# Down projection of a hybrid encoder block: seven block products instead of eight, in four passes of eleven steps

## The chip, the core and the metric

The kernel runs on one NeuronCore of a Trainium2 chip. The metric is the device time of one execution in microseconds (us), and the median of several executions counts.

## What is computed

One layer of a hybrid encoder: norm, input projection, sliding window attention beside a diagonal state space branch, a gated merge, then a gated feed-forward network with a short causal convolution, and a last norm. Everything is float32, 2048 tokens, width 1024, inner width 2816. The change is in the last line of the feed-forward network:

```python
def conv_ffn(h, w_up, conv_w, conv_b, w_down):
    z = causal_dwconv(h @ w_up, conv_w, conv_b)
    val, gate = jnp.split(z, 2, axis=-1)
    return (jax.nn.gelu(gate) * val) @ w_down      # (2048 x 2816) @ (2816 x 1024)
...
x = x + conv_ffn(rms_norm(x, norm_ffn[l]), w_up[l], conv_w[l], conv_b[l], w_down[l])
return rms_norm(x, norm_final)
```

## The kernel before

All tokens are done in two blocks of 1024 (`blk` 0 and 1), one after the other. There is no scheduler: each engine (PE, DVE, ACT, POOL and the SP queue) has its own program, written out by hand in order, and the engines wait for one another through counting semaphores.

**Three products for one.** Each float32 operand is split into a high part (a cast to fp32r) and a low part (the rest), and every product is three matmuls, high times high, high times low and low times high (`three`, lines 418 to 420), each 128x128 by 128x512.

**Up phase.** The product with `w_up` already runs with seven block products for eight. Its 22 periods (one per 128 columns of the value and of the gate) hold 84 matmuls each. POOL casts the high parts (`half`, line 685), DVE makes the weight sums (lines 1530 to 1541), the low parts (`slot_low`, line 1550), the sums that leave PSUM (`c11`, `c22`, `c12`, lines 1596 to 1608), the two side taps of the convolution (`near` and `far`, lines 1617 and 1622) and the gated product (`ff_mul`, line 1627). The result of each period, 128x1024, is stored to `ff` in DRAM. In the order of DVE, `c22` must be out before PE may start its last product of the period, `p4`.

**Down phase.** It computes `ff` times `w_down` with all eight products, in two passes (512 tokens each) of 22 items. An item is one 128-row of `w_down` (`w_raw`, 512 KB, loaded in line 523) and one 128x512 piece of `ff` (256 KB, line 530). POOL casts and subtracts the weights (`split`, lines 642 and 644), ACT casts the values (`down_hi`, line 738), DVE subtracts (`down_low`, line 1631), and PE adds 24 matmuls into the eight PSUM banks. Four items may be ready ahead (`wd`, `ff_hi`, `ff_lo` have four buffers each). The last three items of a pass (`CHUNK`) are done bank by bank, so that DVE can add finished banks to the residual (`down_add`, line 1640, 128x1024 each) while PE goes on.

**Beside the down phase.** After its load for item 7 the SP queue issues the residual (4 MB, from `x2`) and, in block 0, the 4 MB of x for block 1. ACT sums the squares of the new x (line 800) and DVE scales it (`norm_x`, lines 1228 to 1236 and 1263) in two halves, behind items 16 and 18. The last norm (`out_root`, `out_scaled`, line 1252) is done for tiles 0 to 3 in pass 1, and for tiles 4 to 7 of block 1 behind the last matmul.

Of the kernel before, what the change touches and what calls it, by code (L numbers as in the profile page):

```python
# [55 lines left out]
PASSES = 2  # L56
ITEMS = PASSES * FT
UNITS = U_FFN + ITEMS
CHUNK = 3
# [28 lines left out]
def build(nc, A):  # L88

    with ExitStack() as ctx:  # L90
# [67 lines left out]
        wd = [(at(f"wd_hi{i}", a, [D], F32R), at(f"wd_lo{i}", a + 4, [D], F32R)) for i, a in enumerate((96, 104, 128, 136))]  # L158
        ff_raw = [act_hi[:, i, 0:HALF].bitcast(F32) for i in range(4)]
        ff_hi = [act_hi[:, HK + i, 0:HALF] for i in range(4)]  # L160
        ff_lo = [act_lo[:, HK + i, 0:HALF] for i in range(4)]
# [136 lines left out]
        ffr_in = [sem(f"ff_loaded{i}") for i in range(4)]  # L298
        ffhi_done = sem("ff_hi_ready")
        ff_ready = sem("ff_ready")  # L300
        x2_in = [sem(f"ffn_residual_loaded{i}") for i in range(4)]
        d_used = sem("down_item_used")
        dn_done = sem("down_tile_done")
# [47 lines left out]
        def banks(n):  # L351

            return 3 * (n % 2), 3 * (n % 2) + 1, 3 * (n % 2) + 2

# [127 lines left out]
        def _(sp):  # L482
# [36 lines left out]
            def load_down(blk, i, c, k0):  # L519

                sp.wait_ge(raw_free[c % 2], i * 2 + (blk * (UNITS // 2) + U_FFN // 2 + c // 2))
                src = A["wu"][bass.ds(i * 4 + (U_DN + c - k0), 1)].rearrange("u p n -> (u p) n")
                sp.dma_start(w_raw[c % 2][:, :], src).then_inc(raw_in[c % 2], 16)

            def load_ff(blk, i, c, p):

                if not isinstance(i, int) or c >= 4:
                    sp.wait_ge(ff_ready, i * 4 + (blk * ITEMS + c - 3))
                src = A["ff"][bass.ds(i * 4 + (c - p * FT), 1)].rearrange("u p t -> (u p) t")[:, p * HALF:(p + 1) * HALF]
                sp.dma_start(ff_raw[c % 4], src).then_inc(ffr_in[c % 4], 16)  # L530

            def ffn_traffic(blk):
# [12 lines left out]
                def period(i, c):  # L545
                    sp.wait_ge(*item(slot_ready, W22, blk, i, c))
                    load_pair(i, c + 2)
                    if not isinstance(i, int) or c:
                        store_ff(blk, i, c - 1)
                period(0, 0)  # L550
# [5 lines left out]
                load_down(blk, 0, 0, 0)  # L556
                load_down(blk, 0, 1, 0)
                store_ff(blk, 0, FT - 3)
                sp.wait_ge(*item(prod_done, W11, blk, 0, FT - 1))
                for k in range(4):  # L560
                    sp.wait_ge(ff_st[k % 2], 16 * (blk * (FT // 2) + k // 2 + 1))
                    load_ff(blk, 0, k, 0)
# [1716 lines left out]
```

## Time and profile before

| | |
|---|---|
| median of 3 runs | 2584.61 us (2581.55 to 2585.11) |
| the profiled execution | 2581.78 us, span of its instructions 2580.0 us |
| PE busy | 2507.2 us, 97% of the span, 11906 matmuls |
| DVE, ACT, POOL busy | 1527.3, 727.8 and 959.6 us |
| DMA | 298.53 MB, mean 116 GB/s |
| down phase, block 0 and 1 | from 1059 to 1312 us and from 2329 to 2570 us |

The span runs from the first to the last instruction. Matmuls overlap in the pipeline: a row shows some 390 ns for one of 128x512, while one starts every 0.227 us. What the kernel gains or loses is therefore read from the gaps of PE and from the number of its matmuls.

### The profile page before, as it was taken

Reading aid. Unit: us, or ns where it says so; the run is one execution under the profiler, and the core shown is the slowest. Engines: PE = TensorE matmul, PEld = TensorE weight load, DVE = VectorE, ACT = ScalarE, POOL = GpSimd, SP = SyncE. Lnnn points to the kernel's source line nnn. Section 1 sums busy time; section 2 is a strip of 40 time slices with the busy share of each in tenths; the row PEclk is TensorE's granted clock in tenths of the full one; section 3 lists DMA queues with packets and bytes.
Section 4 is the critical chain, followed back from the end, with each engine's and each line's share of the span. In section 5 each row is a group of like instructions: output and inputs, shape, how many; then the busy total and the mean of one; then the engine's idle time right before and its main releaser. Section 6 shows DMA issues by size and latency. Waiting matters only on the chain.

```text
span 2580.0 us, 34191 instructions
## 1 busy us (share of the span) xinstructions
PE 2507.2 (97%) x11906; PEld 2058.2 (80%) x11906; DVE 1527.3 (59%) x2209; ACT 727.8 (28%) x1413; POOL 959.6 (37%) x667
## 2 busy tenths in 40 slices
PE   6999999999999999989999999999999999999998
PEld 5777788888888888868878878888878888888886
DVE  6945455546888888537230235556378888884253
ACT  4035213312333323221121351142133333331111
POOL 2322222350333333567722222225313333336684
PEclk9999999999999999999999999999999999999999
DMA  6242342442121222564412123324312212225452
GB/s 197 88 107 86 131 152 78 147 183 78 66 82 73 89 81 85 183 223 170 147 40 94 54 98 135 127 106 147 155 58 90 81 73 89 81 90 216 147 192 106
DMA packets 117356, 298.53 MB, mean 116 GB/s; under 512 B 18136, under 2 KB 35320, under 8 KB 117256
## 3 DMA queue, kind: packets, MB, share of 16 engines
q1 hardware_dynamic: 79408, 217.37, 23.8%
q10 hardware_dynamic: 37848, 79.80, 8.9%
q8 instruction: 66, 1.08, 0.2%
q14 instruction: 34, 0.28, 0.0%
HBM read 228.45 MB, written 68.68 MB: 115 GB/s over the span
## 4 chain that ended last, share of the span: by engine, by line
PE 87%; DVE 7%; DMA 2%; ACT 2%; POOL 1%; issue 1%; SPq 1%; ACTq 0%; POOLq 0%; DVEq 0%
PE ps L418 27%; PE ps L420 27%; PE ps L419 26%; DMA act_hi<-ff 1%; POOL wd_lo L644 1%; PE ps L1991 1%; PE ps L1977 1%; DVE act_lo L1243 1%; PE ps L1926 1%; PE ps L1915 1%; PE ps L1994 1%; PE ps L1992 1%; PE ps L1837 0%; DVE glu_y L1485 0%; DVE set_t_b L1305 0%
## 5 line engine op out<-in xcount | busy, mean ns | idle before, releaser
L642 POOL CAST w_hi<-w_raw 128x1024 fp32r<-128x1024 f32 x72 | 78.2, 1086 | 744.2 <-PE ps L420 729.2
L685 POOL CAST slot_hi<-pair_raw 128x512 fp32r<-128x512 f32 x220 | 175.9, 804 | 476.0 <-PE ps L420 430.9
L418 PE MATMUL ps<-act_hi,w_hi 128*128 128x512 f32 x832 | 334.3, 402 | 14.4 <-DVE act_lo L1243 7.5
L420 PE MATMUL ps<-act_hi,w_lo 128*128 128x512 f32 x832 | 327.1, 393 | 0.0
L419 PE MATMUL ps<-act_lo,w_hi 128*128 128x512 f32 x832 | 326.2, 392 | 0.0
L418 PE MATMUL ps<-wd_hi,act_hi 128*128 128x512 f32 x704 | 274.7, 390 | 12.1 <-DVE act_lo L1631 12.1
L418 PE MATMUL ps<-act_hi,slot_hi 128*128 128x512 f32 x704 | 274.2, 390 | 0.3 <-DVE slot_lo L1550 0.3
L420 PE MATMUL ps<-wd_hi,act_lo 128*128 128x512 f32 x704 | 274.3, 390 | 0.0
L419 PE MATMUL ps<-wd_lo,act_hi 128*128 128x512 f32 x704 | 274.3, 390 | 0.0
L420 PE MATMUL ps<-act_hi,slot_lo 128*128 128x512 f32 x704 | 273.9, 389 | 0.0
L419 PE MATMUL ps<-act_lo,slot_hi 128*128 128x512 f32 x704 | 273.9, 389 | 0.0
L1631 DVE TENSOR_TENSOR act_lo<-act_hi 128x512 fp32r<-128x512 f32 x88 | 114.4, 1310 | 249.2 <-ACT act_hi L738 249.1
L644 POOL TENSOR_TENSOR wd_lo<-w_raw,wd_hi 128x1024 fp32r<-128x1024 f32 x88 | 236.4, 2687 | 7.0
L418 PE MATMUL ps<-tw_hi,slot_hi 128*128 128x512 f32 x528 | 206.3, 391 | 1.6 <-ACT part L738 1.4
L420 PE MATMUL ps<-tw_hi,slot_lo 128*128 128x512 f32 x528 | 205.5, 389 | 0.0
L419 PE MATMUL ps<-tw_lo,slot_hi 128*128 128x512 f32 x528 | 205.4, 389 | 0.0
L418 PEld LDWEIGHTS ps<-act_hi,w_hi 128*128 128x128 f32 x832 | 157.8, 190 | 51.4 <-DVE act_lo L1243 8.6
L685 POOL CAST slot_hi<-sums 128x512 fp32r<-128x512 f32 x84 | 119.0, 1416 | 206.2 <-DVE sums L1530 108.6
L420 PEld LDWEIGHTS ps<-act_hi,w_lo 128*128 128x128 f32 x832 | 157.7, 190 | 34.4
L644 POOL TENSOR_TENSOR w_lo<-w_raw,w_hi 128x1024 fp32r<-128x1024 f32 x72 | 182.2, 2531 | 5.8
L419 PEld LDWEIGHTS ps<-act_lo,w_hi 128*128 128x128 f32 x832 | 158.0, 190 | 31.2
L418 PEld LDWEIGHTS ps<-wd_hi,act_hi 128*128 128x128 f32 x704 | 132.5, 188 | 40.4 <-DVE act_lo L1631 12.9
(326 smaller groups left out, 4872.4 us busy)
## 6 DMA issues: line engine op xcount, KB each, us to landing
w_raw<-in_wu SPq DMA_DIRECT2D x176, 512.0 KB, 3.5
pair_raw<-in_wu SPq DMA_DIRECT2D x88, 512.0 KB, 3.9
ff<-z SPq DMA_DIRECT2D x44, 512.0 KB, 2.6
act_hi<-ff SPq DMA_DIRECT2D x88, 256.0 KB, 3.7
gates<-junk ACTq DMA_DIRECT2D x64, 256.0 KB, 2.0
sig<-gates ACTq DMA_DIRECT2D x32, 512.0 KB, 4.9
tbl_o<-tables ACTq DMA_DIRECT2D x32, 384.0 KB, 3.4
tbl_r<-tables ACTq DMA_DIRECT2D x32, 256.0 KB, 2.7
```

What stands on the lines that cost most here:

```text
L418: nc.tensor.matmul(out, lh, rh, start=first, stop=False, skip_group_check=onto)
L419: nc.tensor.matmul(out, lh, rl, start=False, stop=False, skip_group_check=onto)
L420: return nc.tensor.matmul(out, ll, rh, start=False, stop=last, skip_group_check=onto)
L642: nc.gpsimd.tensor_copy(hi, w_raw[b][:, :]).then_inc(hi_made, 1)
L644: nc.gpsimd.tensor_tensor(lo, w_raw[b][:, :], f(hi), ALU.subtract).then_inc(w_ready, 1)
L685: nc.gpsimd.tensor_copy(slot_hi[j][:, :, :], src).then_inc(slot_half[KIND[j]], 1)
L1243: stt(act_lo[:, k, cols], ps[:, 4 + n % 4, :], gain[:, k:k + 1], f(act_hi[:, k, cols]), ALU.mult, ALU.subtract).then_inc(act_ready, 1)
L1631: tt(ff_lo[c % 4], ff_raw[c % 4], f(ff_hi[c % 4]), ALU.subtract).then_inc(ff_ready, 1)
L1915: ins = nc.tensor.transpose(ps[:, 6 + j // 4, (j % 4) * P:(j % 4 + 1) * P], logit[i % 2][:, j, :], ident[:, :])
L1926: ins = mm(ps[CH * g:CH * g + CH, 2 + i % 2, par * 256:(par + 1) * 256], vv, rhs, start=True, stop=True)
L1977: ins = mm(ps[SS * g:SS * g + SS, s_bank[m % 2], ri * P:(ri + 1) * P], tbl_r[m % NR][:, TB_W + ri * P + SS * g:TB_W + ri * P + SS * g + SS ...
L1991: mm(o, s_h[b][:, 0, 0:NCH], tab[:, out_v:out_v + 256], start=True, stop=False)
```

## The change

The eight block products of the down phase become seven. The 1024 tokens of a block are split into early and late (512 each), the 22 rows of `w_down` into 11 pairs of an even and an odd row, and its columns into left and right. A **step** is one pair in one pass. With A11, A12 the early values of the even and odd row, A21, A22 the late ones, and B11 to B22 the weights alike:

| pass | steps | products | value sums by DVE | loads of a step |
|---|---|---|---|---|
| 0 | 0 to 10 | A11 B11 and A12 B21 | none | 4 pieces, 1 MB |
| 1 | 11 to 21 | S2 T2 and S1 T1 | S1 = A21 + A22, S2 = S1 - A11 | 5 pieces, 1.25 MB |
| 2 | 22 to 32 | S3 T3 and S4 B22 | S3 = A11 - A21, S4 = A12 - S2, from three operations | 6 pieces, 1.5 MB |
| 3 | 33 to 43 | A22 T4 | none | 2 pieces, 0.5 MB |

A piece is 128x512 (256 KB). The weight sums T1 = B12 - B11, T2 = B22 - T1, T3 = B22 - B12 and T4 = B21 - T2 are the same for both blocks: DVE makes them in the up phase of block 0, two operations behind each period's `slot_low` of the last slot, from rows that SP loads for it, and SP stores them to `tw` in DRAM. The raw buffers of a step are three deep, the operands four deep, and they now lie over all of `act_hi` and `act_lo`. POOL only casts, and DVE makes the low parts of the weights too. Products accumulate in banks 0 to 3 and 4 to 7 through the passes; DVE adds them to the residual in 28 half tiles of 128x512. `CHUNK` is 2, and its unit is now a bank.

```diff
+            def load_step(blk, t):
+                n, j = t // PAIRS_K, t % PAIRS_K
+                b = t % 3
+                if t >= 3:
+                    sp.wait_ge(step_ready, operands_by(blk, t - 3))
...
+                for dst, src in pairs:
+                    sp.dma_start(dst, src).then_inc(step_in[b], 16)
...
+                def down_t(i, c):                       (SP, up phase of block 0)
...
+                    if c:
+                        sp.wait_ge(t_done, i * 4 + 2)
+                        store_t(i, 1)
+                        store_t(i, 2)
+                    elif not isinstance(i, int) or i:
+                        sp.wait_ge(t_done, i * 4)
+                        store_t(i - 1, 0)
+                        store_t(i - 1, 3)
+                        sp.wait_ge(t_st, i * 64)
...
+                        load_t(i, c)
...
+                sp.wait_ge(*item(prod_done, S1, blk, 0, FT - 1))
+                load_step(blk, 0)
+                sp.wait_ge(*item(prod_done, S3, blk, 0, FT - 1))
+                load_step(blk, 1)
+                load_step(blk, 2)
...
+                    load_step(blk, t)
+                    if blk + 1 < BLOCKS and 5 <= t < 9:
+                        load_x(sp, blk + 1, t - 5, t - 4)
+                    if 9 <= t < 13:
+                        j = t - 9
+                        sp.dma_start(xres[:, 2 * j:2 * j + 2, :], x2[:, 2 * j:2 * j + 2, :]).then_inc(x2_in[j], 16)
...
+                for t in range(STEPS):                  (POOL)
+                    if t == 0:
+                        pool.wait_ge(*item(prod_done, W12, blk, 0, FT - 1))
+                    elif t == 2:
+                        pool.wait_ge(*item(prod_done, W22, blk, 0, FT - 1))
+                    elif t >= 4:
+                        pool.wait_ge(d_used, blk * STEPS + t - 3)
+                    pool.wait_ge(step_in[t % 3], loads_by(blk, t))
+                    for n in range(products(t)):
+                        nc.gpsimd.tensor_copy(d_hi[t % 4][n], raw_w[t % 3][:, n, :]).then_inc(d_half, 1)
...
+                def step_lows(t):                       (DVE)
+                    value_sums(t + 1)
+                    for n in range(products(t)):
+                        dve.wait_ge(d_half, halves_by(blk, t) - products(t) + n + 1)
+                        tt(d_lo[t % 4][n], raw_w[t % 3][:, n, :], f(d_hi[t % 4][n]), ALU.subtract).then_inc(step_ready, 1)
...
+                        tt(f_lo[t % 4][n], value_of(t, n), f(f_hi[t % 4][n]), ALU.subtract).then_inc(step_ready, 1)
...
+                for t in range(3, STEPS):
+                    step_lows(t)
+                    if blk + 1 < BLOCKS and t in (7, 9):
+                        norm_x(blk + 1, (t - 7) // 2)
+                    if t in (12, 23, 34):
+                        for n in range(8 * (t // PAIRS_K) - 8, 8 * (t // PAIRS_K)):
+                            bank_add(n)
+                    if t == 36:
+                        out_root(blk, 0, 4, out_parts(blk))
+                    if 36 <= t < 40:
+                        out_scaled(t - 36)
```

**DVE, behind the last slot of an up period.** Before (`slot_lo_148` is the low part of the fourth sum, the two z rows are `near` and `far`):

```order
L1608 TENSOR_TENSOR pre_157<-part_155,ps 128x512
L1550 TENSOR_TENSOR slot_lo_148<-pair_raw_152,slot_hi_141 128x512
L1617 SCALAR_TENSOR_TENSOR z_159<-pre_157,conv_v_185,z_159 128x1024
L1622 SCALAR_TENSOR_TENSOR z_159<-pre_157,conv_v_185,z_159 128x1024
```

and with the change, in block 0 (`down_t_row` and `down_t_164` hold the rows of `w_down`):

```order
L1680 TENSOR_TENSOR pre_157<-part_155,ps 128x512
L1622 TENSOR_TENSOR slot_lo_148<-pair_raw_152,slot_hi_141 128x512
L1708 TENSOR_TENSOR down_t_row<-down_t_row 128x512
L1709 TENSOR_TENSOR down_t_row<-down_t_164,down_t_row 128x512
L1689 SCALAR_TENSOR_TENSOR z_159<-pre_157,conv_v_186,z_159 128x1024
L1694 SCALAR_TENSOR_TENSOR z_159<-pre_157,conv_v_186,z_159 128x1024
```

Two operations of 128x512 have come in between `slot_low` and `near`.

**DVE, one and a half steps of pass 2, with the change** (`step_f` and `step_w` are the raw values and weights of a step, a number of the buffer behind them; before, an item had one row here, `act_lo<-act_hi`):

```order
L1728 TENSOR_TENSOR step_f_168<-step_f_168 128x512
L1729 TENSOR_TENSOR step_f_168<-step_f_168 128x512
L1731 TENSOR_TENSOR step_f_168<-step_f_168 128x512
L1737 TENSOR_TENSOR act_lo<-step_w_170,act_hi 128x512 x2
L1740 TENSOR_TENSOR act_lo<-step_f_167,act_hi 128x512 x2
L1728 TENSOR_TENSOR step_f_166<-step_f_166 128x512
```

The three sums of the next step (buffer 168) stand ahead of the four low parts of this one (buffers 170 and 167).

## Rows read from the trace of the kernel before

**Rows 1.** Page, costliest groups: busy us, mean ns, idle before and its releaser

```profile
L418 PE MATMUL ps<-wd_hi,act_hi 128*128 128x512 f32 x704 | 274.7, 390 | 12.1 <-DVE act_lo L1631 12.1
L1631 DVE TENSOR_TENSOR act_lo<-act_hi 128x512 fp32r<-128x512 f32 x88 | 114.4, 1310 | 249.2 <-ACT act_hi L738 249.1
```

**Rows 2.** Timeline of ACT, two items: start, length, idle before

```profile
1164.82 0.63 ACT L738 ACTIVATE act_hi<-act_hi 128x512 fp32r<-128x512 f32 x1 [3.37 <-PE ps L420]
1170.26 0.63 ACT L738 ACTIVATE act_hi<-act_hi 128x512 fp32r<-128x512 f32 x1 [4.81 <-PE ps L420]
```

**Rows 3.** Stretches of 4 us, block 0: PE, PEld, DVE, ACT, POOL, PEclk, DMA, GB/s

```profile
1100.00:1104.00 4.00, 2.92 (x13) 2.07 (x12) 0.00 (x0) 0.00 (x0) 0.00 (x0) 1.00 1.03 410
1104.00:1108.00 4.00, 0.00 (x0) 0.00 (x0) 0.00 (x0) 0.00 (x0) 0.00 (x0) 0.85 1.02 408
...
1112.00:1116.00 4.00, 1.88 (x5) 1.49 (x6) 3.51 (x2) 0.63 (x1) 3.56 (x3) 0.50 0.32 99
```

**Rows 4.** Chain of waits, block 0: start, length, what

```profile
1095.75 14.82 DMA act_hi<-ff
...
1115.34 0.43 PE ps L420
```

**Rows 5.** Stretches of 4 us, block 1, same columns

```profile
2373.00:2377.00 4.00, 3.14 (x15) 2.39 (x14) 2.50 (x2) 0.13 (x1) 3.57 (x3) 1.00 0.52 189
```

**Rows 6.** Operations by line: ns min, median, max; first and last start

```profile
L1550 DVE TENSOR_TENSOR slot_lo<-pair_raw,slot_hi x220: 671/681/1104, 563.3 to 2317.6; 128x512 fp32r<-128x512 f32 x110
L685 POOL CAST slot_hi<-sums x84: 617/1478/1485, 648.1 to 2303.1; 128x512 fp32r<-128x512 f32 x84
```

**Rows 7.** DMA issues by line: KB each, median us to landing

```profile
w_raw<-in_wu SPq DMA_DIRECT2D x176, 512.0 KB, 3.5
pair_raw<-in_wu SPq DMA_DIRECT2D x88, 512.0 KB, 3.9
ff<-z SPq DMA_DIRECT2D x44, 512.0 KB, 2.6
```

**Rows 8.** Timelines of DVE and ACT around the norm of the new x

```profile
1147.11 1.04 ACT L800 ACTIVATE junk<-xnext 128x1024 bf16<-128x1024 f32 x1
1148.26 1.28 ACT L738 ACT_TABLE_LOAD   x1
1148.27 0.17 DVE L1228 TENSOR_SCALAR var_x<-ssq_x 128x4 f32<-128x4 f32 x1 [2.60 <-ACT junk L800]
1152.77 5.74 DVE L1263 TENSOR_SCALAR xnext<-xnext,rstd_x 128x1024 f32<-128x1024 f32 x4
```

**Rows 9.** Operations by line: the scaling of x, ns min, median, max

```profile
L1263 DVE TENSOR_SCALAR xin<-xin,rstd_x x12: 745/749/2879, 14.5 to 1166.5; 128x1024 f32<-128x1024 f32 x12
```

**Rows 10.** Timelines of the up phase: DVE and SP in one period

```profile
808.16 0.36 SPq L517 DMA_DIRECT2D ff<-z  x1
811.00 0.69 DVE L1603 TENSOR_TENSOR pre<-part,ps 128x512 f32<-128x512 f32 x1 [0.78 <-issue]
814.43 0.69 DVE L1550 TENSOR_TENSOR slot_lo<-pair_raw,slot_hi 128x512 fp32r<-128x512 f32 x1
816.07 1.28 DVE L1617 SCALAR_TENSOR_TENSOR z<-pre,conv_v,z 128x1024 f32<-128x1024 f32 x1 [0.94 <-ACT z L1083]
```

**Rows 11.** A stretch of 50 us of the up phase, columns as in rows 3

```profile
800.00:850.00 50.00, 50.00 (x223) 41.39 (x222) 42.72 (x54) 15.23 (x26) 18.22 (x19) 1.00 0.25 94
```

**Rows 12.** Timeline of PE: its last matmul of the down phase

```profile
2569.86 0.39 PE L420 MATMUL ps<-wd_hi,act_lo 128*128 128x512 f32 x1
```

**Rows 13.** Timeline of DVE behind it: last add, its norm, last scaling

```profile
2570.36 1.22 DVE L1640 TENSOR_TENSOR xres<-xres,ps 128x1024 f32<-128x1024 f32 x1 [0.21 <-PE ps L420]
2571.50 0.15 DVE L1228 TENSOR_SCALAR var_out<-ssq_out 128x1 f32<-128x1 f32 x1
2574.14 0.15 DVE L1228 TENSOR_SCALAR var_out<-ssq_out 128x1 f32<-128x1 f32 x1
2575.58 1.28 DVE L1252 SCALAR_TENSOR_TENSOR xres<-xres,rstd_out,gfin 128x1024 f32<-128x1024 f32 x1
```

More of the change, by code:

```diff
@@ L55 @@
 U_DN = U_UP + 2 * FT
[L56 to L59, printed above, removed]
+UNITS = U_FFN
+PAIRS_K = FT // 2
+PASSES = 4
+STEPS = PASSES * PAIRS_K
+CHUNK = 2
 W11, W12, S1, S2, S3, S4, W22 = range(7)
@@ L1148, in period @@
                     else:
-                        for k in range(4):
-                            down_hi(0, k)
+                        value_hi(0)
                     value_out_pair(i, c)
@@ new lines, in value_sums @@
+                def value_sums(t):
+                    if t >= STEPS or not sums_of(t):
+                        return
+                    made = sums_by(blk, t)
+                    a, b, c, d = (raw_f[t % 3][:, n, :] for n in range(4))
+                    dve.wait_ge(step_in[t % 3], loads_by(blk, t))
+                    if sums_of(t) == 2:
+                        tt(a, a, b, ALU.add).then_inc(step_sum, 1)
+                        dve.wait_ge(step_sum, made + 1)
+                        tt(c, a, c, ALU.subtract).then_inc(step_sum, 1)
+                    else:
+                        tt(a, a, c, ALU.subtract).then_inc(step_sum, 1)
+                        tt(b, b, d, ALU.subtract).then_inc(step_sum, 1)
+                        dve.wait_ge(step_sum, made + 2)
+                        tt(b, b, a, ALU.add).then_inc(step_sum, 1)
@@ L1858, in proj @@
                         pe.wait_ge(proj_evac, blk * 2 * N_IN + (3 if n == 3 else n - 1))
+                    if blk and n < 3:
+                        pe.wait_ge(dn_evac, blk * ADDS)
                     if n in (12, 13):
@@ L2195, in _, with down_bank @@
-                for c in range(FT + 1, 24):
-                    down_item(0, c)
-                with pe.Fori(6, 10) as i:
-                    for c in range(4):
-                        down_item(i, c)
-                for c in range(40, ITEMS - CHUNK):
-                    down_item(0, c)
-                down_last(1)
+                def down_bank(t, n, q, first, last):
+                    tok = slice(q * P, (q + 1) * P)
+                    b = t % 4
+                    return three(ps[:, 4 * n + q, :], f_hi[b][n][:, tok], f_lo[b][n][:, tok], d_hi[b][n], d_lo[b][n],
+                                 first, last, onto=t // PAIRS_K not in ((0,), (0, 1))[n])
```

356 lines of the change are left out of this document (176 added, 180 removed).

## The prediction

> **What bounds the kernel now.** I read the page first: PE is busy for 97% of the span, so time can only come from fewer matmuls or from PE's gaps. Then the groups: all waits of PE ahead of the down phase's matmuls come to 12.1 us, and DVE's 88 low parts stand idle for 249 us waiting for casts [rows 1]. So in the down phase everything but PE waits, and PE sets the pace. That pace is read off ACT, whose cast waits until PE has freed a buffer: one item every 1170.26 - 1164.82 = 5.44 us [rows 2]. An item has 24 matmuls, so one matmul starts every 0.2267 us.
>
> The gaps come next. In block 0 DMA runs at 408 to 410 GB/s while PE stops at 1102.9 us [rows 3]. The chain names a single transfer of values, 14.8 us long: it is queued behind the 8 MB of residual and new x [rows 4]. Of the 12.1 us, 0.9 belong to block 1 [rows 5], so 11.2 to this gap. Behind it the granted clock reads 0.50, that is 1.2 GHz [rows 3], and matmuls take 0.43 us each [rows 4], which costs about 2 us more.
>
> **What goes.** Before, 2 x 1056 matmuls; now 33 steps of 24 and 11 of 12, 924 a block. So 264 fewer: 264 x 0.2267 = **59.8 us**. The gap of 11.2 us, its 2 us of slow clock and the 0.9 us of block 1 go too (**14.1 us**), since x and residual are now loaded 1 MB at a time between step loads. From step 5 to 12 a step asks for 2.1 to 2.4 MB, 5.1 to 5.8 us at 410 GB/s against 5.44; the steps by then ready cover that.
>
> **What comes: the work of DVE.** A subtraction of 128x512 takes 0.68 us, pipelined 0.61, and up to 1.10 us when it meets a cast of POOL; the cast takes 0.62 us at least and 1.48 us when it meets DVE [rows 6]. So the two take turns: I count them as one resource. The Trainium skill (SBUF — State Buffer, section on the shared port pair) says so too: a DVE operation with two SBUF inputs and a GpSimd operation exclude each other for a whole instruction. By the rows alone they could still miss one another in part, and that is the lower bound below.
>
> A step of pass 1 is 6 DVE operations and 2 casts: 6 x 0.61 + 2 x 0.6 = 4.9 us, with two dependent waits 5.2. Pass 2 has 7 operations: 5.8 at worst, 5.2 if some casts fall into gaps. There is a second tie. `value_sums(t + 1)` stands ahead of the low parts of step t, and the load of step t + 1 starts only when step t - 2 is ready. So two steps cost one landing plus one step of DVE. A 512 KB load lands in 3.5 us [rows 7], of which 1.3 are transfer at 410 GB/s, so 2.2 are fixed; 1.31 MB land in 5.4 us, 1.57 MB in 6.0. The period is (5.4 + 5.4)/2 = 5.4 us in pass 1 and (6.0 + 5.5)/2 = 5.7 in pass 2, where PE wants 5.44. And at the end of each pass DVE also adds eight half tiles (8 x 0.65, 5 us) while its next step waits. For eleven steps DVE needs 11 x 5.4 + 5 = 64.4 us in pass 1 and, with some of the adds under landings, about 65 in pass 2; PE needs 59.8. The last two steps of a pass must both be ready, so lead is eaten there. That is 4.6 and 5 us a block, **19 us** in all, waited mostly ahead of steps 20 and 31. Nearest bound below: casts in the gaps, 0. Bound above: 0.75 us for each operation and a step on every landing, 15 us a block. I take the middle, as every piece of it has a row.
>
> **The head.** Before, four items could be ready. Now steps 2 and 3 lie over operands that PE reads until its last up product, and step 1 loads only when the S3 product is done, 5.6 us ahead of step 0 (two products of 12 matmuls). It lands at -1 us, but DVE still has `ff_mul`, `c12`, `near` and `far` of the last period between the low parts of steps 0 and 1: about 5.5 us, then four low parts. Stepping the order forward gives step 1 ready at 8.8 us in block 0 (with its two T sums) and 7.6 in block 1, where PE asks at 5.4: **5.6 us** together. At best 1, at worst 8.
>
> **The norm of the new x, block 0.** One half is four squares of ACT (1.04 us each, with their reads 1.13), a table load of 1.28 us the first time, six small DVE operations, and four scalings that took 5.74 us beside POOL's subtractions [rows 8] but take 0.75 us each alone [rows 9]. So a half holds DVE for 4.3 us, and the first for 8 with the wait for ACT. Before, DVE idled 2.8 us an item on average (249.2/88, [rows 1]). Now both halves stand inside steps 7 to 10, after the loads of x have used up the lead (step 7 is ready only some 2 us early). From step 7 to 10 DVE needs 8 + 4.3 + 3 x 2.8 + 1.4 us of sums = 22 us; PE, wanting 9 and 10 together, gives it 2 + 2 x 5.44 = 13. **10 us** of waiting, ahead of steps 8 and 9; bounds 5 and 15.
>
> **Clock.** A gap of 7 us is likely to bring the slow clock again: it cost 2 us behind the gap of 11 [rows 3, 4]. I put 3 us for all gaps; bounds 0 and 8.
>
> **The tail.** Before, PE's last matmul ends at 2570.1 [rows 12] and the span 9.9 us later: one add of 1.22 us, two norms of 2.64 us, a store [rows 13]. Finished tiles came 4.08 us apart (18 matmuls). Now they come 1.36 us apart (6 matmuls), and a norm still takes 2.64. With E the end of PE: adds at E - 4.0 and E - 2.6, norm until E + 0.7, add, norm until E + 4.0, add, norms until E + 7.3 and E + 9.9, store 3.1. The tail is 13.0: **+3.1 us**.
>
> **The up phase of block 0.** Two operations of DVE come into each of 22 periods of 84 x 0.2267 = 19.0 us. They stand ahead of `near`, which waits 0.94 us there anyway [rows 10]. In even periods they wait for rows that SP loads only after its stores of sums have landed: SP is free at 808.5, two stores more land by 812.2 (512 KB land in 2.6 us [rows 7]), the rows 4.2 us later at 816.4, where DVE would ask at 815.1 [rows 10]. So `near` moves by 1.7 us. Behind it DVE waits 0.78 us ahead of `c22` [rows 10], and PE wants `c22` only after one more product, 2.7 us, of which `c22` takes 0.69. Slack 2.8, need 1.7: hidden; **2 us** for jitter and the first period, bounds 0 and 8. The additional traffic, 2 MB in two periods, 55 GB/s, runs beside 94 GB/s [rows 11] and costs nothing.
>
> **Sum.** Profiled execution 2581.8 us: - 59.8 - 14.1 + 19 + 5.6 + 10 + 3 + 3.1 + 2 = - 31.2, so 2550.6. That execution lies 2.8 us below the median of the runs, so I say **2551 us**. A measurement of this kernel tells 0.2% (5 us) from no change.
>
> A page speaks against the change. Rows show reads at 408 to 410 GB/s [rows 3]. The Trainium skill (DMA: Bandwidth & Descriptors, "Where 436 GB/s comes from") says that between HBM and SBUF some 360 GB/s bind. By its figure the 1.57 MB alone would take 4.4 us, an estimate, and the sum would come out near rival 2.
>
> **Rivals.**
> 1. *All cover holds* (0.14). Casts fall between DVE's operations, so only the norm (9 us) and 2 us of the head are left: 2581.8 - 73.9 + 11 + 1 + 3 + 1 = 2524. For it: DVE has a median of 0.68, not 0.9, in the up phase beside POOL [rows 6].
> 2. *The loads are the bound* (0.18). Values and weights come in rows of 2 KB instead of 4, three to four transfers a step. If a landing takes 0.6 to 0.8 us longer, both passes' periods grow by 0.35 us: 22 steps in each of two blocks, 15 us, and 2 more at the norm: 2568. For it: steps 5 to 12 already need 94% and more of the time at 410 GB/s. Against: nothing else is in the queue in pass 2.
> 3. *Slower, through the up phase* (0.07). If the rows land 2 us later than I said, DVE's wait for them delays `c22` past its 2.8 us of slack, and PE stands in `p4`. It decides from a delay of `near` of 3 us on, and to end above 2590 it has to cost 1.8 us in each of 22 periods. DVE is then busy or blocked for over 19.0 us a period; it was busy 42.72 of 50, so 16.2 [rows 11], and the two operations add 1.3.
> 4. *Slower, through DVE in passes 1 and 2* (0.04). It decides from 0.8 us an operation on (every third meets a cast and waits it out): a step takes 6.0 us in pass 1 and 6.8 in pass 2, with the adds 11 and 20 us a block over PE, less 4 of lead, so 54 in place of 19: 2586.
>
> That the change does not do what it says is not open: the matmuls are counted in the program.
>
> **Numbers.** The forecast has 0.57, with a range of its own from 2538 to 2562. Range for 8 in 10: 2528 to 2574, from half of rival 1 to beyond rival 2. Faster 0.88, within 0.2% 0.04, slower 0.08.
>
> **What would show it.** PE: 11642 matmuls, the last one some 13 us ahead of the end. Waits of PE for DVE `act_lo` of 2 to 4 us ahead of step 1, 2 to 10 ahead of steps 8 and 9 of block 0, about 3 ahead of steps 20 and 31 in both blocks. DVE idle in pass 2 until `step_f` lands; `step_f` landing in 5.5 to 6 us. The up phase of block 0 as long as that of block 1 to 2 us. It is wrong if PE waits in the up phase, if DVE's operations in the down phase average over 0.8 us, or if passes 1 and 2 run without a gap.

## The result, and the profile after

The changed kernel takes 2570.44 us (median of 6 runs, 2566.25 to 2574.32), the kernel before in the same job 2584.86 us (6 runs, 2581.55 to 2587.49). The ratio is 0.994, with a 95% interval from 0.9927 to 0.9953. So it is faster by 14.4 us, where 33.6 had been forecast; the time lies inside the range of 2528 to 2574, near its upper end. The profiled execution took 2574.16 us, its span 2572.0. In the job of the last four kernels below one execution of the kernel before took 5130.5 us; it is left out of their ratios.

The first two parts of the page:

```profile
span 2572.0 us, 33476 instructions
PE 2470.1 (96%) x11642; PEld 2020.2 (79%) x11642; DVE 1714.0 (67%) x2623; ACT 760.8 (30%) x1479; POOL 771.6 (30%) x645
```

PE has the 11642 matmuls of the forecast. The waits of PE in the down phase of block 0 (1071.9 to 1312.5 us) and then of block 1 (2330.2 to 2558.9), by the view of waits (who waited, for what: us in total, times, longest):

```profile
PE ps L466 <- DVE act_lo L1740: 20.1, 5, 7.3
...
PE ps L466 <- DVE act_lo L1740: 11.7, 4, 6.2
PE ps L466 <- DVE xres L1756: 1.8, 1, 1.8
```

Before, all such waits came to 12.1 us [rows 1]; now they are 33.6. Of these 31.8 are for the last low part of a step, and 1.8, ahead of step 11 of block 1, for DVE's add (`xres`) that empties the bank which step 11 writes. I placed each by the starts of PE's matmuls (a step is 24 of them, 12 in pass 3). A stop is a stretch between two starts that is over 0.3 us longer than 0.2267, and it counts with what it is longer:

| | block 0 | block 1 |
|---|---|---|
| down phase before | 252.2 | 240.5 |
| after | 240.5 | 228.7 |
| of it matmuls at 0.2267 us | 209.5 | 209.5 |
| stops in all | 22.3 | 14.7 |
| ahead of step 1 | 3.6 | 1.7 |
| ahead of steps 8 to 11 | 7.8 | 2.9 |
| ahead of step 20 | 6.7 | 6.7 |
| ahead of steps 30 and 31 | 4.2 | 3.4 |
| starts at double distance | 7.7 | 3.4 |

The last row is what starts some 0.43 us apart cost over 0.2267; smaller delays make up the missing 1.0 and 1.1 us. The starts at double distance come behind the stops, as here behind the one ahead of step 20 (stretches of 4 us: busy us and count of PE, PEld, DVE, ACT, POOL, then PEclk, DMA share, GB/s):

```profile
1192.00:1196.00 4.00, 4.00 (x20) 3.30 (x19) 2.34 (x4) 0.76 (x2) 0.00 (x0) 1.00 0.93 336
1196.00:1200.00 4.00, 0.54 (x3) 0.11 (x1) 2.50 (x3) 0.00 (x0) 2.08 (x2) 0.94 0.95 325
1200.00:1204.00 4.00, 1.26 (x3) 1.10 (x4) 4.00 (x7) 1.15 (x2) 1.63 (x2) 0.50 0.23 72
1204.00:1208.00 4.00, 4.00 (x14) 3.12 (x14) 3.72 (x6) 1.15 (x2) 0.08 (x1) 0.71 0.98 334
```

After a stop of 6.4 us the granted clock is 0.50, that is 1.2 GHz, and still 0.71 on average in the next stretch: 14 matmuls in 4 us in place of 18.

Why the low parts are late shows in DVE's timeline, for the step of pass 1 behind a load and for the first sums of pass 2 (start, length, idle before and its releaser):

```profile
1184.93 0.69 DVE L1724 TENSOR_TENSOR step_f<-step_f 128x512 f32<-128x512 f32 x1 [1.72 <-DMA step_w<-tw]
1185.65 0.98 DVE L1726 TENSOR_TENSOR step_f<-step_f 128x512 f32<-128x512 f32 x1
1186.56 1.69 DVE L1737 TENSOR_TENSOR act_lo<-step_w,act_hi 128x512 fp32r<-128x512 f32 x2
1188.18 1.28 DVE L1740 TENSOR_TENSOR act_lo<-step_f,act_hi 128x512 fp32r<-128x512 f32 x2
...
1197.46 0.69 DVE L1728 TENSOR_TENSOR step_f<-step_f 128x512 f32<-128x512 f32 x1 [3.13 <-DMA step_w<-in_wu]
```

and in SP's, which issues a load as soon as a step is ready:

```profile
1178.43 0.88 SPq L587 DMA_DIRECT2D step_f<-ff  x2
1179.35 0.43 SPq L587 DMA_DIRECT2D step_w<-tw  x1
...
1189.48 0.88 SPq L587 DMA_DIRECT2D step_f<-ff  x2
```

The load issued at 1178.43 is waited for until 1184.93, 6.5 us; then come two sums and four low parts, and at 1189.48 the step is ready and SP issues the load of the next step but two. That is the two-step tie of the prediction: 11.05 us for two steps, 6.5 of landing and 4.55 of DVE, 5.5 a step, where PE takes 5.44. In pass 2 the issues lie (1259.98 - 1223.94)/6 = 6.0 us apart. The landing had been put at 5.4 us. Two things in the trace go with the difference, and no run separates them: the third transfer is issued 0.92 us behind the first (1178.43 and 1179.35), and the rate climbs slowly. Stretches of 1 us around the issue at 1156.56, whose data DVE takes up at 1162.96:

```profile
1157.00:1158.00 1.00, 1.00 (x6) 0.84 (x5) 0.97 (x3) 0.05 (x1) 0.00 (x0) 1.00 0.41 49
1158.00:1159.00 1.00, 1.00 (x7) 0.81 (x6) 1.00 (x3) 1.00 (x2) 0.00 (x0) 1.00 0.80 172
1159.00:1160.00 1.00, 1.00 (x6) 0.84 (x5) 1.00 (x3) 0.11 (x1) 0.00 (x0) 1.00 1.00 326
1160.00:1161.00 1.00, 1.00 (x6) 0.82 (x5) 0.27 (x1) 0.00 (x0) 0.00 (x0) 1.00 1.03 379
```

Two more places. In the up phase of block 0 PE now waits for `c22` (L1675), and DVE for the rows of the weight sums; the view of waits from 660 to 1071 us:

```profile
PE ps L466 <- DVE pre L1675: 3.8, 7, 0.7
...
DVE down_t_row L1708 <- DMA down_t<-in_wu: 28.5, 10, 3.3
```

That up phase takes 438.5 us; before it took 432.1, as the one of block 1 does in both kernels. By the starts of the matmuls 6.1 of the 6.4 us are stops of 0.1 to 1.0 us in nine periods, none of them in two periods running. And the tail: the last matmul starts at 2558.67, and DVE's last scaling is here, where [rows 13] had 2575.58:

```profile
2558.67 0.39 PE L468 MATMUL ps<-act_hi,act_lo 128*128 128x512 f32 x1
```
```profile
2567.61 1.28 DVE L1324 SCALAR_TENSOR_TENSOR xres<-xres,rstd_out,gfin 128x1024 f32<-128x1024 f32 x1
```

The parts add up. Down phases: -23.5; up phase of block 0: +6.4; tail 13.1 us in place of 9.9: +3.2; between the phases -0.5. That is -14.4, the difference of the medians. (Ahead of the first up phase the profiled execution is 6.3 us longer than the one before, though the program is the same there; with it the two spans differ by 8.0 us. Over all kernels below that phase starts between 626.8 and 634.2 us, so it is left out of the sum. That the rest meets the difference of the medians so exactly is in part chance.)

### The profile page after: what moved, and what is told of

The parts are those of the page before. It is cut to its first block, busy times and chain, and to the rows that moved or that the text cites. A ratio compares the mean times of both kernels' runs of the same rounds, so it can differ in the third digit from the quotient of the medians.

```text
span 2572.0 us, 33476 instructions
## 1 busy us (share of the span) xinstructions
PE 2470.1 (96%) x11642; PEld 2020.2 (79%) x11642; DVE 1714.0 (67%) x2623; ACT 760.8 (30%) x1479; POOL 771.6 (30%) x645
## 4 chain that ended last, share of the span: by engine, by line
PE 68%; DVE 17%; DMA 7%; issue 3%; ACT 2%; SPq 1%; POOL 1%; DVEq 0%; ACTq 0%; POOLq 0%
PE ps L466 21%; PE ps L468 20%; PE ps L467 20%; DMA step_w<-in_wu 3%; DMA step_w<-tw 2%; DVE act_lo L1737 2%; DVE act_lo L1740 2%; DMA down_t<-in_wu 1%; SPq L587 1%; DVE slot_lo L1622 1%; PE ps L2097 1%; DVE act_lo L1315 1%; PE ps L2083 1%; DVE z L1699 1%; POOL slot_hi L764 1%
## 5 line engine op out<-in xcount | busy, mean ns | idle before, releaser
L764 POOL CAST slot_hi<-pair_raw 128x512 fp32r<-128x512 f32 x220 | 183.8, 842 | 419.5 <-PE ps L468 325.0
L466 PE MATMUL ps<-act_hi 128*128 128x512 f32 x616 | 247.1, 401 | 33.6 <-DVE act_lo L1740 31.8
L467 PE MATMUL ps<-act_lo,act_hi 128*128 128x512 f32 x616 | 244.8, 397 | 0.0
L468 PE MATMUL ps<-act_hi,act_lo 128*128 128x512 f32 x616 | 244.1, 396 | 0.0
L805 POOL CAST act_hi<-step_w 128x512 fp32r<-128x512 f32 x154 | 139.0, 926 | 341.4 <-DMA step_w<-in_wu 155.3
L813 ACT ACTIVATE act_hi<-step_f 128x512 fp32r<-128x512 f32 x154 | 89.4, 624 | 329.0 <-DVE step_f L1731 101.0
L466 PEld LDWEIGHTS ps<-act_hi 128*128 128x128 f32 x616 | 118.6, 193 | 64.9 <-DVE act_lo L1740 38.9
```

The lines of the kernel that those rows point to most:

```text
L466: nc.tensor.matmul(out, lh, rh, start=first, stop=False, skip_group_check=onto)
L467: nc.tensor.matmul(out, lh, rl, start=False, stop=False, skip_group_check=onto)
L468: return nc.tensor.matmul(out, ll, rh, start=False, stop=last, skip_group_check=onto)
L764: nc.gpsimd.tensor_copy(slot_hi[j][:, :, :], src).then_inc(slot_half[KIND[j]], 1)
L805: nc.gpsimd.tensor_copy(d_hi[t % 4][n], raw_w[t % 3][:, n, :]).then_inc(d_half, 1)
L813: ins = nc.scalar.activation(out, in_, kw.pop("func", ACT.Identity), **kw)
```

## The experiments

Three questions: what makes the waits in passes 1 and 2 (the tie, the landings, DVE's work or its meeting with POOL); what makes those ahead of steps 8 and 9; what makes the first up phase longer. Ratios are to the kernel before, run in the same job; the phases are from each run's trace, to be held against 240.5 and 228.7 us for the down phases and 438.5 for the up phase.

**No weight sums.** `down_t` is not called and the step loads take plain rows of `w_down`, so the weight sums are left out of the computation.

```
-                    if blk == 0:
-                        down_t(i, c)
...
-(raw_w[b][:, :, :], tmade[:, 0:2, :])
+(raw_w[b][:, :, :], wide[:, :, HALF:])
```

> Leaves out the weight sums T1 to T4: their loads, their DVE operations and their stores in the up phase of block 0, and every step loads plain rows of w_down of the same size instead (so the down products are of other weights). Theory A (the loads of those rows land after DVE asks for them, so DVE is late for c22 and PE waits 0.5 to 0.9 us in every second period): the up phase of block 0 falls from 438.5 us to the 432.1 us of block 1, its seven gaps of PE inside the loop go, the head of the down phase of block 0 waits 1.5 us less at step 1, and the whole is 6 to 9 us faster than the change. Rival (the two operations themselves fill DVE, or the stores disturb the loads of the next pair): the same sum, but then PE's gaps would not stand in every second period alone. Both phases down are otherwise as they are: PE waits at steps 8, 9, 20 and 31.

Measured: 2554.64 us (4 runs, 2549.78 to 2558.19), ratio 0.9877 (0.9854 to 0.99). The up phase of block 0 is back at 432.2: the sums and what hangs on them cost the whole 6.4 us there. The down phases take 233.6 and 226.9, with 3.3 and 6.0 us ahead of step 20 (6.7 in both blocks with the sums), 3.3 and 2.8 ahead of step 31 and 8.0 ahead of step 9. So the waits of passes 1 and 2 do not hang on the rows in DRAM that hold the sums, though the one ahead of step 20 of block 0 is halved: a load issued at 1158.36 is taken up at 1164.37, 6.0 us later in place of 6.4 to 6.5, and two steps take 10.6 us in place of 11.05.

**Casts on ACT.** The 154 casts of a step's weights are made by ACT in place of POOL.

```
-                        nc.gpsimd.tensor_copy(d_hi[t % 4][n], raw_w[t % 3][:, n, :]).then_inc(d_half, 1)
+                        copy(d_hi[t % 4][n], raw_w[t % 3][:, n, :], d_half, 1)
```

> The casts of the weights in the down phase are done by ACT ahead of those of the values; POOL does nothing there. Theory B (DVE's operations with two inputs in SBUF and POOL's casts take turns, and that makes a step of passes 1 and 2 longer than PE's 5.44 us): DVE's low parts of the weights fall from 0.84 us mean to 0.64, PE's waits ahead of steps 20 (6.4 us in both blocks) and 31 (3.3) go, steps 8 and 9 of block 0 keep 7 to 9 us, the slow clock costs 2 to 4 us in place of 11: 22 to 30 us faster than the change, ratio to before 0.983 to 0.986. Rival C (the landing of the loads sets the period, DVE's length does not matter): waits at 20 and 31 stay within 1 us, under 6 us faster. Rival D (ACT becomes late instead, four casts of 0.63 us and its own waits): PE waits for ACT or for DVE behind ACT, no gain.

Measured: 2548.31 us (4 runs, 2545.45 to 2552.07), ratio 0.9854 (0.9835 to 0.9873); down phases 231.7 and 218.7. Ahead of step 20 stand 1.6 us in both blocks, ahead of step 31 2.6 and 2.5, and 2.1 and 1.9 are new ahead of step 22, where PE waits for the adds that empty its banks. DVE by line, from 1126 to 1260 us in the changed kernel (two rows), and from 1120 to 1260 with the casts on ACT (two rows); busy us and mean ns, then idle before and its releaser:

```profile
L1729 DVE TENSOR_TENSOR step_f<-step_f 128x512 f32<-128x512 f32 x10 | 9.7, 972 | 0.0
L1728 DVE TENSOR_TENSOR step_f<-step_f 128x512 f32<-128x512 f32 x10 | 7.3, 729 | 11.0 <-DMA step_w<-in_wu 11.0
```
```profile
L1721 DVE TENSOR_TENSOR step_f<-step_f 128x512 f32<-128x512 f32 x11 | 7.6, 692 | 0.4
L1718 DVE TENSOR_TENSOR step_f<-step_f 128x512 f32<-128x512 f32 x11 | 7.6, 691 | 15.6 <-DMA step_w<-in_wu 15.6
```

The second sum falls from 0.97 to 0.69 us. The Trainium skill (SBUF — State Buffer, "Who interferes with whom") says that a DVE instruction with two SBUF inputs contends with a GpSimd instruction that reads SBUF. That fits: without POOL's casts every group of DVE's sums and low parts has a mean of 0.68 to 0.69 us here. But DVE does not stop waiting for loads; it idles longer before them (15.6 us in place of 11.0 on that line). A shorter step of DVE shortens the circle of landing and step; that this is the way in which it helps is my reading, and the order of sums moved below bears it out.

**Four deep.** A fourth buffer for a step's raw values and weights; a load waits for the step four back. POOL's weight splits of block 1 wait until the last step of block 0 is ready, since the buffer lies over theirs.

```
-(96, 128, 136))]
+(96, 128, 136, 184))]
...
-                if t >= 3:
-                    sp.wait_ge(step_ready, operands_by(blk, t - 3))
+                if t >= 4:
+                    sp.wait_ge(step_ready, operands_by(blk, t - 4))
```

> A fourth raw buffer for the values and weights of a step (in the place of the weight buffers that the down phase does not use), so that the load of step t waits for step t - 4 and not t - 3. Nothing else. Theory C (value_sums(t + 1) stands ahead of the low parts of step t, so that with three buffers two steps cost one landing and one step of DVE): the waits at steps 20 and 31 of both blocks go, 9 us a block with what the clock adds, about 20 us faster than the change. Theory B alone (DVE and POOL need over 5.44 us a step whatever the loads do): the waits shrink by under a third, under 7 us faster. If both are needed at once, since the period is their sum, this and the run with the casts on ACT each take the waits away.

Measured: 2538.42 us (4 runs, 2537.07 to 2541.68), ratio 0.9818 (0.98 to 0.9836); down phases 226.1 and 212.7. No stop is left ahead of steps 20 and 31 in either block; ahead of steps 8 and 9 of block 0 there are still 2.1 and 6.5 us. So DVE, with all its operations and its meetings with POOL, keeps up with PE in passes 1 and 2 once it need not wait for loads.

**The last four steps bank by bank.** In pass 3 four steps share a bank in place of two, so that tiles finish farther apart.

```
+                    chunk = 4 if p == 3 else CHUNK
-                    if t % PAIRS_K < PAIRS_K - CHUNK:
+                    if t % PAIRS_K < PAIRS_K - chunk:
```

> In pass 3 alone the last four steps are done bank by bank, in place of the last two, so that finished banks come 2.72 us apart and not 1.36. Theory (the tail of 13.1 us is DVE's row of norms, 2.64 us a tile with an add of 0.6, that starts late): DVE has done two norms by the end of PE, the tail falls to about 10.5 us, 2 to 3 us faster than the change. Rival (four steps must be ready at once at step 40, which PE waits for): the gain is eaten by a new wait of 2 to 5 us ahead of step 40 in both blocks, so slower by up to 6 us.

Measured: 2583.08 us (10 runs, 2575.62 to 2588.02), ratio 0.999 (0.9977 to 1.0002). The tail falls from 13.1 to 10.4 us (tiles now 12 matmuls apart), but PE stops 4.7 and 4.9 us ahead of step 40 in block 0 and 1: all four steps must be ready at once. The last of them, step 43, waits for its load and not for a free operand. In block 0 PE has left step 39's operands at 1301.5; the load, issued at 1300.34 when step 40 was ready, releases POOL's cast at 1303.82. The tail's 2.7 us cost 9 and more.

**Weight sums behind near and far.**

```
-                    if blk == 0:
-                        down_t(i, c)
                     near(0, i, c)
                     far(0, i, c)
+                    if blk == 0:
+                        down_t(i, c)
```

> The two DRAM-bound weight sums of a period stand behind near and far on DVE in place of ahead of them; nothing else is changed. My theory: the first up phase is 6.4 us longer than the second because the sums wait ahead of near for their rows, and near pushes c22 past its slack. Then the up phase of block 0 falls from 438.5 to 432 to 433 us, and the time from 2570 to about 2564. Rival: the two more operations or the 2 MB more of traffic in two periods cost the time by themselves, wherever they stand; then the up phase of block 0 stays at 437 to 439 us and the time at 2570.

Measured: 2565.28 us (4 runs, 2560.59 to 2569.16), ratio 0.9912 (0.9889 to 0.9935); up phase of block 0 433.2 us. The same operations and the same traffic cost 1.1 us in place of 6.4. The view of waits from 660 to 1067 us: PE now waits once for `c22`.

```profile
PE ps L466 <- DVE pre L1675: 0.8, 1, 0.8
```

**Sums of values behind the low parts.** One line of DVE's order is moved.

```
                 def step_lows(t):
-                    value_sums(t + 1)
                     for n in range(products(t)):
...
                         tt(f_lo[t % 4][n], value_of(t, n), f(f_hi[t % 4][n]), ...)
+                    value_sums(t + 1)
```

> On DVE the sums of values of step t + 1 stand behind the low parts of step t in place of ahead of them; nothing else is changed. My theory: in passes 1 and 2 the load of step t + 1 starts only when step t - 2 is ready, and step t is ready only when step t + 1 has landed, so that two steps cost a landing of 6.4 us and a step of DVE. With that tie cut the waits of PE ahead of steps 20 and 31 shrink from 6.4 and 3.3 us in each block to under 2 each, and the wait ahead of step 9 of block 0 shrinks too: 2554 to 2560 us. Rival: DVE has too much to do in these passes beside the casts (six or seven operations a step, eight adds at the end of a pass). Then the waits stay within 1 us of what they were and the time at 2567 to 2571.

Measured: **2533.70 us** (4 runs, 2532.42 to 2538.84), ratio 0.9802 (0.9781 to 0.9824), 20 us better than the best that I had expected. The down phases take 223.5 and 212.0 us, stops 10.0 and 1.9 us, starts at double distance 3.3 and 0. Waits of PE in the down phase of block 0, then block 1:

```profile
PE ps L466 <- DVE act_lo L1739: 8.7, 3, 4.7
...
PE ps L466 <- DVE act_lo L1739: 1.5, 1, 1.5
```

DVE's timeline in pass 2, one step:

```profile
1187.02 0.68 DVE L1728 TENSOR_TENSOR step_f<-step_f 128x512 f32<-128x512 f32 x1
1187.62 0.68 DVE L1729 TENSOR_TENSOR step_f<-step_f 128x512 f32<-128x512 f32 x1
1188.33 0.69 DVE L1731 TENSOR_TENSOR step_f<-step_f 128x512 f32<-128x512 f32 x1
1189.53 1.67 DVE L1736 TENSOR_TENSOR act_lo<-step_w,act_hi 128x512 fp32r<-128x512 f32 x2 [0.51 <-POOL act_hi L805]
1191.12 1.28 DVE L1739 TENSOR_TENSOR act_lo<-step_f,act_hi 128x512 fp32r<-128x512 f32 x2
1192.33 0.68 DVE L1728 TENSOR_TENSOR step_f<-step_f 128x512 f32<-128x512 f32 x1
```

A step takes 1192.33 - 1187.02 = 5.3 us, and DVE never waits for a load. From 1124 to 1246 us the first sums of both passes stood idle for

```profile
L1724 DVE TENSOR_TENSOR step_f<-step_f 128x512 f32<-128x512 f32 x11 | 9.2, 833 | 1.9 <-DMA step_w<-tw 1.9
L1728 DVE TENSOR_TENSOR step_f<-step_f 128x512 f32<-128x512 f32 x11 | 9.1, 830 | 0.0
```

1.9 us, where the changed kernel has 21.8 (10.8 on L1724 and 11.0 on L1728, 1126 to 1260 us). The landings are no shorter: by the view of DMAs a 512 KB transfer of `step_f` takes 5.1 us here and 4.7 there. So for the waits ahead of steps 20, 30 and 31 the tie was the cause, and no resource. The down phases hold 33.7 of the some 36 us gained. With the sums ahead, the low parts of step t wait for load t + 1, which is issued when step t - 2 is ready; the three buffers work like two. With the sums behind, they wait for load t, issued when step t - 3 is ready.

**Norm later.** Its halves stand at steps 14 and 18 on ACT and DVE.

```
-                    if blk + 1 < BLOCKS and t in (7, 9):
+                    if blk + 1 < BLOCKS and t in (14, 18):
```

> The two halves of the norm of the new x stand at steps 14 and 18 in place of 7 and 9, for ACT and DVE both; the loads stay where they are. The forecast's theory: the norm holds DVE while PE waits ahead of steps 8 and 9 of block 0. Then the wait of 7.5 us ahead of step 9 falls under 2 us and, with its slow clock, the time by about 9 us to 2561, unless the norm then costs the same ahead of step 20. Rival: the wait comes from the 8 MB of x and residual between the step loads of steps 5 to 12. Then 5 to 7 us stay ahead of steps 8 to 10, the wait ahead of step 20 of block 0 grows by 2 to 4 us, and the time is 2568 to 2575.

Measured: 2575.28 us (7 runs, 2568.22 to 2578.38), ratio 0.9952 (0.9936 to 0.9969), no better than the changed kernel. The wait ahead of step 9 is 9.3 us in place of 7.8, with no norm near it, and 3.2 us come in ahead of steps 19 and 22. The norm was not what stopped PE at step 9; the rival holds.

**Loads spread, norm later.** As before, and the eight loads of 1 MB stand ahead of steps 5, 7, ... 19.

```
-                    if blk + 1 < BLOCKS and 5 <= t < 9:
+                    if blk + 1 < BLOCKS and t in (5, 7, 13, 15):
...
-                    if 9 <= t < 13:
+                    if t in (9, 11, 17, 19):
```

> As the run before, and the eight loads of 1 MB of x and residual stand in front of every second step (5, 7, 9, 11, 13, 15, 17, 19) in place of eight steps in a row. If the burst of loads makes the wait ahead of step 9, it falls under 2 us here and not in the run before, and the down phase of block 0 becomes 8 to 12 us shorter than that of the changed kernel (240.5): 2560 us. If the norm alone made it, this run and the one before are alike. A part may come back ahead of step 20, where loads of pass 1 now share the queue with x.

Measured: 2563.15 us (4 runs, 2562.56 to 2567.65), ratio 0.9916 (0.9895 to 0.9936), down phase of block 0 236.8 us. The wait ahead of step 9 falls from 9.3 to 4.0. That part of it is the burst of loads; what is left had not been expected.

**Both orders.** 

> Both moves of DVE's order together: the sums of values of step t + 1 behind the low parts of step t, and the two DRAM-bound weight sums behind near and far. The two causes lie in different phases, so the gains should add: the down phases as with the first move alone (223.5 and 212.0 us), the up phase of block 0 at 433 us as with the second alone; 2533.7 - 5 = about 2528.5 us. Rival: with the first up phase shorter the stores of sums run into the next loads and a part comes back; over 2532.

Measured: 2537.42 us (4 runs, 2535.02 to 2537.7), ratio 0.9806 (0.9785 to 0.9827). The up phase of block 0 takes 433.2 us, as expected, the down phases 225.2 and 212.2; yet the time is that of the order of sums alone, within the interval. In the two traces the 5.3 us gained in the up phase stand against 6.9 us more ahead of it (the phase starts at 633.7 us here and at 626.8 there), where the programs are the same, and 1.7 us in the down phase of block 0, where the wait ahead of step 1 is 5.2 us in place of 2.8. The 6.9 us lie in the first 200 us, and the granted clock differs there. The same stretch of 4 us with the sums alone moved, then with both:

```profile
134.00:138.00 4.00, 2.88 (x14) 2.21 (x13) 3.97 (x2) 1.36 (x3) 0.00 (x0) 1.00 0.71 231
```
```profile
134.00:138.00 4.00, 4.00 (x21) 4.00 (x20) 3.93 (x3) 2.48 (x5) 1.44 (x1) 0.50 0.38 109
```

One program takes several times there, so a gain of 5 us can hide in the start of an execution; that it varies between executions of one kernel, and not between kernels, is likely but not shown, as each was traced once.

**Loads spread and the head moved, on top.** The two moves just tried, and step 1's casts and low parts (`value_hi(1)`, `step_lows(1)`) ahead of `near` and `far` of the last period.

> As the run before, and three moves more: the loads of x and residual in front of every second step from 5 to 19, the two halves of the norm at steps 14 and 18, and step 1's casts and low parts ahead of near and far of the last period. Left in the down phase of block 0 are the waits ahead of step 1 (2.8 us), of steps 8 and 9 (1.5 and 4.9) and 3.3 us of slow clock. If those at 8 and 9 come from the burst of loads they go, and with them the slow clock: down phase of block 0 at 212 to 214 us, the time at 2517 to 2520. If it is the norm, they move to steps 15 to 19: 2525 to 2529.

Measured: 2536.38 us (4 runs, 2529.61 to 2538.35), ratio 0.9798 (0.9771 to 0.9825): nothing gained. Both waits moved. The one ahead of step 1 (5.2 us in block 0) is now ahead of step 2 (4.9). Step 2's load is not late (issued at 1061.46, step 0 starts at 1065.9) and its casts are done by 1072.1; but in DVE's order its low parts stand behind `near`, `far` and the weight sums, and end at 1081.4. Those ahead of steps 8 and 9 are gone, and 6.6 us stand ahead of steps 19 to 22, where the norm and the late x loads are; 2.8 of them are waits for the adds of pass 1, which DVE reaches late. With three buffers and POOL's casts the new x costs about 6 us in block 0 wherever it is put.

**The last three steps bank by bank, on top.** As the run with four, with 3.

> As the run before, and in pass 3 of a block the last three steps run bank by bank in place of two, so that finished tiles come 9 matmuls apart (2.0 us) in place of 6 (1.4). If the order of DVE's sums was what made the steps of pass 3 late in the run with four such steps, no new wait comes ahead of step 41 and the tail falls from 13.1 to about 11.8 us: 1 to 1.5 us less than the run before. If loads are late by themselves there, a new gap of 2 us or more ahead of step 41 in both blocks makes it 2 to 5 us longer.

Measured: 2538.73 us (4 runs, 2537.16 to 2542.87), ratio 0.9812 (0.9791 to 0.9833). New stops of 2.7 and 2.0 us ahead of step 41 in both blocks, though DVE's order is mended. The load is the limit here too. Step 43's, into one of three raw buffers, is issued at 1279.08; PE has left the operands of step 39 at 1280.06; and POOL's cast for step 43 waits for the load:

```profile
1283.42 0.61 POOL L806 CAST act_hi<-step_w 128x512 fp32r<-128x512 f32 x1 [2.69 <-DMA step_w<-tw]
```

**Four deep and casts on ACT, on top of the spread loads.**

> As the run with spread loads and the moved head, and a fourth buffer for a step's loads and the casts of weights on ACT in place of POOL. If what was wrong with passes 1 and 2 was the tie of two steps alone, nothing is left there for a buffer or for a free port to give: within 0.1% of that run. If a little of the wait ahead of steps 8 and 9 is left there, up to 3 us less.

Measured: **2521.23 us** (4 runs, 2518.97 to 2522.76), ratio 0.9749 (0.9727 to 0.977), the best of all. Down phases 212.9 and 210.1 us of which 209.5 are matmuls. All that is left of PE's waits in them, block 0:

```profile
PE ps L466 <- DVE act_lo L1731: 2.0, 2, 1.3
```

I had expected 0 to 3 us less than with spread loads alone; it is 15, of which 11.7 in block 0 and 3.4 in block 1. Two things were changed at once, but where the time goes shows in DVE's rows. Ahead of step 2 stand 1.5 us in place of 4.9, and step 2's load is issued no earlier than before (4.3 us ahead of step 0 here, 4.4 there). What is shorter is DVE's work: from the start of step 0's low parts to the end of step 2's it takes 15.5 us in place of 18.4, with POOL's casts gone from beside it. Step 2's low parts of the weights, with spread loads alone and here:

```profile
1078.12 2.11 DVE L1737 TENSOR_TENSOR act_lo<-step_w,act_hi 128x512 fp32r<-128x512 f32 x2
```
```profile
1072.91 1.29 DVE L1728 TENSOR_TENSOR act_lo<-step_w,act_hi 128x512 fp32r<-128x512 f32 x2
```

Around the second half of the norm it is the same: from the sums ahead of it to the adds of pass 1 DVE takes 27.7 us in place of 31.2 (1157.30 to 1184.99, 1167.30 to 1198.50), and in neither run does it wait more than 0.4 us for loads there. So once the order is mended and the loads are spread, DVE's time sets the wait in the head and behind the norm, and there its meetings with POOL cost. What the fourth buffer gives beside that, no run shows alone.

## Why the prediction was wrong, and where it was right

By its own steps, in us, measured from the same two traces. The mechanisms were mostly right, and two terms were far too small: the slow clock (+3, measured +11.1) and the up phase of block 0 (+2, measured +6.4).

| step | forecast | measured |
|---|---|---|
| 264 fewer matmuls | -59.8 | -59.8 (239.4 to 209.5 a block) |
| gap of before, its clock, block 1 | -14.1 | -13.7 |
| DVE and loads in passes 1 and 2 | +19 | +21.0 (steps 20, 30, 31) |
| head, step 1 | +5.6 | +5.3 |
| norm of the new x | +10 | +7.8 at steps 8 and 9, +2.9 in block 1 |
| slow clock | +3 | +11.1 |
| tail | +3.1 | +3.2 |
| up phase of block 0 | +2 | +6.4 |
| small ones | 0 | +1.4 |
| sum | -31.2 | -14.4 |

**The clock** is the step that failed most: 8 of the 16.8 us. I priced it as one gap, from the 2 us behind the gap of 11 us [rows 3, 4], and added one for the rest. By the starts at double distance, the stops of the changed kernel brought 2.4 us (behind the stop of 3.2 us at step 1), 1.2 (behind 7.5), 1.6 (behind 6.4) and 2.4 (behind 3.3) in block 0, and 2.0 (behind 6.4) and 1.4 (behind 3.4) in block 1; those of 0.6 to 2 us brought none. A stop of 3 us had the price of one of 7, and the one of 11 before had 1.0, where the prediction had read 2. So the number of longer stops counted, not their sum. The down phases of all 14 traces say so too: none of 51 stops of 0.5 to 1.95 us brought any; of 36 between 1.95 and 3.5 us 13 brought none and the others 0.2 to 2.4; each of 30 longer ones brought 1.0 to 2.4, and those of over 6 us no more than those of 3.5 to 6. With the order of sums mended, 10.0 us of stops bring 3.3 us of it in block 0, and 1.9 us none in block 1. Behind the term stands a second slip: it was made for gaps as a whole, while the waits had been forecast one by one, at seven places.

**The up phase** was mis-sized by 4.4 us. The mechanism stands in rival 3: the rows come late, `near` moves, `c22` misses its slack. The slack was taken as 2.8 us; in the changed kernel DVE's wait for the rows takes 2.9 us on average over ten periods and up to 3.3, where `near` had been forecast to move by 1.7, and PE then stops for `c22` in every second period. The move behind `far` shows that the place was the cause.

**Passes 1 and 2** came out near the sum, by luck of two errors. The landing of pass 1 was put at 5.4 us and was 6.4 to 6.5. DVE's step was put at 5.4 us in the same period (its own count had been 4.9 to 5.2), and was 4.55 in the pair of steps above; with no load to wait for it takes 3.7 to 5.0 us in pass 1 and 4.8 to 5.6 in pass 2. The two errors cancel: a period of 5.5 us against 5.4. And I said that DVE's work and the tie share the wait. Of the waits ahead of steps 20, 30 and 31 the runs show the tie alone: one line moved takes them away, with every operation and every meeting with POOL still there. I had named the tie and had not asked what the time would be without it.

**The norm** was the wrong cause for a nearly right size. Moving it took nothing away ahead of step 9 (9.3 us in place of 7.8); spreading the loads did (4.0), the order of the sums alone hardly (6.7 ahead of steps 8 and 9), and with both nothing was left. Part of that wait is the burst of step loads and 8 MB of x and residual, which had been counted as covered by the steps already ready. And block 1, with only the residual, waits 2.9 us there, which the forecast had at nothing. 2.0 of them stand ahead of step 11, where PE waits for the first add of pass 0; DVE, itself held up by loads (7.5 us for the first of pass 1), comes to it only at 2394.16. With the sums moved behind 0.3 us of it are left.

**Right:** the matmuls, the head, the tail, the old gap, and the places of all waits but those of `c22` and of that add. **Rival 2** (2568 us, landings longer by 0.6 to 0.8) came nearest to the time, and landings were longer, by 1 us; but its cause, loads as the bound, falls for passes 1 and 2: with as many bytes in less time nothing waits there. From 1126 to 1250 us the mended order moves 33.4 MB at a mean of 269 GB/s; the changed kernel moves 33.6 MB from 1126 to 1260 at 251. **Rival 1** (2524 us, all cover holds) has about the time of the last run, which changes order, loads, buffers and casts to get there. **Rival 4** falls: an operation of DVE takes 0.76 us on average in the changed kernel and 0.77 with the mended order, in the stretches shown, with means by line of 0.68 to 0.97, and DVE keeps up. **The page against the change:** the Trainium skill (DMA: Bandwidth & Descriptors, "Where 436 GB/s comes from") has some 360 GB/s as what binds between HBM and SBUF. That is again not borne out: the view of DMAs of the mended order shows slices of 385 to 398 GB/s from 1126 us on.

## What to carry to other kernels

When work for a later step is placed ahead of work for this one on an in-order engine, count how many buffers are left between the load and its first reader: the wait stands where the first reader stands, and here it made three buffers work like two, at a price of some 36 us. Price the slow clock by the number of longer stops (here 1.0 to 2.4 us for each of over 3.5 us, and nothing for those under 2), not by their length. Before a wait is put down to an engine's load, ask for how long that engine itself idles, and for whom: DVE idled 21.8 us for loads in the very stretch in which it was held to be too busy. And look again once the wait is gone: with the order mended it was DVE's time, stretched beside POOL, that was left in the head and behind the norm.

## What was not expected of the hardware

A load of 1.31 MB in three transfers took 6.3 to 6.6 us from its first issue to its reader where no earlier load was under way, and 7.5 where one was. In the one shown the traffic is at 49, 172 and 326 GB/s in stretches of 1 us that begin 0.4, 1.4 and 2.4 us behind its first issue, and only then at some 380; its third transfer is issued 0.9 us behind the first. So its time is not 2.2 us and the bytes at 410 GB/s; taken that way it comes out 1 us short. And a stop of PE of some 4 us cost as much slow clock as one of 6 to 11.
